# Start of a float32r transformer block on one core: loads in halves, another order of splits and products, eight warming products

## The reference

```
xn   = rms_norm(h, norm1)
proj = xn @ w_in            # q, k, v, z, b, a, sc_c, sc_u, sc_b, gate_a, gate_b
...
q, k, v = split(silu(causal_conv(concat(q, k, v))))
o    = chunk_gated_delta_rule(l2(q), l2(k), v, g, beta)
y_a  = (rms_norm(o) * silu(z)) @ w_dn_out
y_b  = (sc_b * causal_conv(sc_c * sc_u)) @ w_sc_out
h    = h + (sigmoid(gate_a) * y_a + sigmoid(gate_b) * y_b) @ w_o
gt, up = split(rms_norm(h, norm2) @ w_gate_up)
out  = rms_norm(h + (silu(gt) * up) @ w_down, final_norm)
```

## Time and profile before

| | us |
|---|---|
| median of 3 runs | 1045.04 (1044.47 to 1045.52) |
| profiled execution | 1045.25 |
| its span, first to last instruction | 1043.4 |
| TensorE busy | 1028.6 (99%) |
| VectorE, ScalarE, GpSimd busy | 638.4, 486.9, 471.0 |
| mean granted TensorE clock | 0.997 |

### The profile page before, as it was taken

How to read it: one execution, slowest core, us unless ns; L and a number is a source line. 1 busy time by engine, 2 the same in 40 slices (tenths; PEclk the granted TensorE clock), 3 DMA queues, 4 the chain that set the end, 5 groups by cost and what they waited for, 6 DMA issues and landing times.

```text
span 1043.4 us, 22623 instructions
## 1 busy us (share of the span) xinstructions
PE 1028.6 (99%) x9025; PEld 924.2 (89%) x9025; DVE 638.4 (61%) x1141; ACT 486.9 (47%) x1069; POOL 471.0 (45%) x403
## 2 busy tenths in 40 slices
PE   9999999999999999999999999999999999999996
PEld 8989899999999998978888888879999999988886
DVE  6575766767566757563321112699999999972103
ACT  7735454453545353542422233555455555653322
POOL 0163636354454536362554655642322222455553
PEclk9999999999999999999999999999999999999998
DMA  6222212121222121122253233212332332332312
GB/s 230 73 77 73 78 62 78 65 84 63 84 68 75 63 92 63 62 66 78 82 180 121 81 101 101 98 65 96 107 117 94 116 104 100 121 106 97 101 61 81
DMA packets 28825, 95.61 MB, mean 92 GB/s; under 512 B 2984, under 2 KB 5288, under 8 KB 28720
## 3 DMA queue, kind: packets, MB, share of 16 engines
q1 hardware_dynamic: 27520, 91.77, 26.4%
q10 hardware_dynamic: 1200, 2.38, 0.6%
HBM read 92.03 MB, written 2.11 MB: 90 GB/s over the span
## 4 chain that ended last, share of the span: by engine, by line
PE 90%; DVE 5%; ACT 2%; issue 1%; DMA 1%; DVEq 0%; SPq 0%; ACTq 0%
PE bank L1388 90%; DVE pair_sums L1247 1%; DVE og_lo L1226 1%; DVE w_lo L1250 0%; DMA h_in<-h_t 0%; DVE cv L1076 0%; ACT w_hi L529 0%; DVE og_lo L1219 0%; DMA h_in<-gc_dram 0%; PE bank L1588 0%; PE bank L1582 0%; DVE h L1197 0%; DVE raw L905 0%; DVE c L1265 0%; DVE bank L1207 0%
## 5 line engine op out<-in xcount | busy, mean ns | idle before, releaser
L428 POOL TENSOR_TENSOR w_lo<-w_raw,w_hi 128x512 fp32r<-128x512 f32 x202 | 274.6, 1373 | 341.9 <-ACT w_hi L529 341.8
L1388 PE MATMUL bank<-x_hi,w_hi 128*128 128x258 f32 (+2 forms) x896 | 247.6, 334 | 0.4 <-DVE raw L905 0.2
L1388 PE MATMUL bank<-x_hi,w_lo 128*128 128x258 f32 (+2 forms) x896 | 230.4, 315 | 0.0
L1388 PE MATMUL bank<-x_lo,w_hi 128*128 128x258 f32 (+2 forms) x896 | 227.9, 315 | 0.0
L529 ACT ACTIVATE w_hi<-w_raw 128x512 fp32r<-128x512 f32 x278 | 166.6, 622 | 89.9 <-PE bank L1388 86.0
L1388 PEld LDWEIGHTS bank<-x_hi,w_lo 128*128 128x128 f32 x896 | 147.3, 189 | 11.1
L1388 PEld LDWEIGHTS bank<-x_hi,w_hi 128*128 128x128 f32 x896 | 146.3, 189 | 12.2 <-DVE w_lo L916 0.6
L1388 PEld LDWEIGHTS bank<-x_lo,w_hi 128*128 128x128 f32 x896 | 146.3, 189 | 8.8
L1388 PE MATMUL bank<-xe,w_hi 128*128 128x256 f32 (+1 forms) x602 | 123.0, 293 | 2.7 <-DVE t L1212 1.8
L1388 PE MATMUL bank<-og_hi,w_hi 128*128 128x256 f32 (+1 forms) x416 | 124.6, 299 | 0.8 <-DVE w_lo L1250 0.6
L1388 PE MATMUL bank<-og_lo,w_hi 128*128 128x256 f32 (+1 forms) x416 | 123.7, 297 | 0.0
(11 more groups left out here) (306 smaller groups left out, 1827.2 us busy)
## 6 DMA issues: line engine op xcount, KB each, us to landing
w_raw<-w_stream SPq DMA_DIRECT2D x140, 512.0 KB, 3.5
cst<-w_stream SPq DMA_DIRECT2D x22, 512.0 KB, 3.5
h_in<-h_t SPq DMA_DIRECT2D x4, 528.0 KB, 7.1
h<-h_t ACTq DMA_DIRECT2D x1, 2048.0 KB, 11.1
h_in<-gc_dram SPq DMA_DIRECT2D x7, 264.0 KB, 3.1
out<-h SPq DMA_DIRECT2D x4, 256.0 KB, 2.9
out<-h SPq DMA_DIRECT2D x2, 384.0 KB, 2.6
cst<-consts SPq DMA_DIRECT2D x1, 512.0 KB, 8.5
```

Of the source, the lines that this page charges most:

```text
L428: nc.gpsimd.tensor_tensor(low_weights(n)[:, at], raw_weights(n)[:, at], high_weights(n)[:, at].bitcast(f32), ALU.subtract).then_inc(wlo_re ...
L1388: return nc.tensor.matmul(o, w, x, start=start, stop=stop)
```

## The change

The first loads are cut: h tiles 0 and 1 come each by itself, the first two weight blocks in halves, in the order small, w0 first half, h0, h1, w1 first half, h 2-3, w0 second half, h 4-5, w1 second half, h 6-7. ACT and DVE make the weight halves in the order (block 0, first), (1, first), (0, second), (1, second), which `FIRST_HALVES` and `first_half` tell to all who wait; ACT puts the x_hi tiles between them. PE makes the high products of k = 0 and 1 before the low ones of the same block and waits for `whi_ready` for the high ones. `WARM` is 8. The numbers of matmuls, copies and bytes are otherwise the same.

```diff
-WARM = 16
+WARM = 8
+FIRST_HALVES = [(0, 0), (1, 0), (0, 1), (1, 1)]
+def first_half(n, half):
+    return FIRST_HALVES.index((n, half)) + 1 if n < 2 else 2 * n + half + 1
...
             if n < 5:
-                engine.wait_ge(wlo_first, 2 * n + half + 1)
+                engine.wait_ge(wlo_first, first_half(n, half))
...
             sp.dma_start(sm[:, :], small[:, :]).then_inc(small_in, 16)
-            for part in range(4):
+            sp.dma_start(w_raw[:, 0, 0:512], w_stream[0, :, 0:512]).then_inc(w_in[0], 16)
+            sp.dma_start(h_in[:, 0, :], h_t[:, 0, :]).then_inc(h_loaded[0], 16)
+            sp.dma_start(h_in[:, 1, :], h_t[:, 1, :]).then_inc(h_second, 16)
+            sp.dma_start(w_raw[:, 1, 0:512], w_stream[1, :, 0:512]).then_inc(w_in[1], 16)
+            for part in range(1, 4):
                 sp.dma_start(h_in[:, 2 * part:2 * part + 2, :], h_t[:, 2 * part:2 * part + 2, :]).then_inc(h_loaded[part], 16)
-                if part == 0:
-                    for n in range(2):
-                        sp.dma_start(w_raw[:, n, :], w_stream[n, :, :]).then_inc(w_in[n], 16)
+                if part < 3:
+                    n = part - 1
+                    sp.dma_start(w_raw[:, n, 512:1024], w_stream[n, :, 512:1024]).then_inc(w_second[n], 16)
...
             def plain_high(k):
-                act.wait_ge(h_loaded[k // 2], 16)
+                act.wait_ge(h_second if k == 1 else h_loaded[k // 2], 16)
...
-                wait_raw_loaded(act, n)
+                if n < 2 and half:
+                    act.wait_ge(w_second[n], 16)
+                else:
+                    wait_raw_loaded(act, n)
...
             act.wait_ge(small_in, 16)
+            split_weights(0, 0)
             plain_high(0)
             plain_high(1)
-            for n in range(2):
-                split_weights(n, 0)
-                split_weights(n, 1)
-            for k in range(2, KT):
+            split_weights(1, 0)
+            plain_high(2)
+            plain_high(3)
+            split_weights(0, 1)
+            plain_high(4)
+            split_weights(1, 1)
+            for k in range(5, KT):
                 plain_high(k)
...
+            def first_low_half(n, half):
+                at = slice(512 * half, 512 * half + 512)
+                dve.wait_ge(whi_ready, first_half(n, half))
...
             dve.wait_ge(small_in, 16)
-            first_low_weights(0)
-            first_low_weights(1)
+            for n, half in FIRST_HALVES:
+                first_low_half(n, half)
             for k in range(KT):
                 plain_low(k)
...
-                for k, n in [(0, 0), (1, 0), (0, 1), (1, 1)] + [(k, n) for k in range(2, KT) for n in range(2)]:
+                def first_products(k, n, w):
                     parts, to = outs(n)
-                    if k % 4 == 0:
+                    if k % 4 == 0 and w is w_hi:
+                        pe.wait_ge(whi_ready, first_half(n, k // 4))
+                    if k % 4 == 0 and w is w_lo:
                         wait_low(pe, n, k // 4)
                     pe.wait_ge(xhi_ready, k + 1)
-                    for w in (w_hi, w_lo):
-                        for o, s in zip(to, parts):
-                            mm(o, w[:, n, k * 128:(k + 1) * 128], x_hi[:, k, s], start=k == 0 and w is w_hi, stop=False)
+                    for o, s in zip(to, parts):
+                        mm(o, w[:, n, k * 128:(k + 1) * 128], x_hi[:, k, s], start=k == 0 and w is w_hi, stop=False)
+                for n in range(2):
+                    for w in (w_hi, w_lo):
+                        first_products(0, n, w)
+                        first_products(1, n, w)
+                for k in range(2, KT):
+                    for n in range(2):
+                        first_products(k, n, w_hi)
+                        first_products(k, n, w_lo)
```

More of the change, by code:

```diff
@@ L263, in hybrid_block_kernel @@
         h_loaded = [sem(f"h_loaded{part}") for part in range(4)]
+        h_second = sem("h_second")
+        w_second = [sem(f"w_second{n}") for n in range(2)]
         w_in = [sem(f"w_in{slot}") for slot in range(4)]
@@ L909, in plain_low @@
                                                x_hi[:, k, :].bitcast(f32), ALU.mult, ALU.subtract).then_inc(xlo_ready, 1)
-            def first_low_weights(n):
[L911 to L917, removed]
+            def first_low_half(n, half):
+                at = slice(512 * half, 512 * half + 512)
+                dve.wait_ge(whi_ready, first_half(n, half))
+                if n >= 2:
+                    dve.wait_ge(block_done, n - 1)
+                nc.vector.tensor_tensor(w_lo[:, n % 2, at], w_raw[:, n % 3, at], w_hi[:, n % 2, at].bitcast(f32),
+                                        ALU.subtract).then_inc(wlo_first, 1)
+            def first_low_weights(n):
+                first_low_half(n, 0)
+                first_low_half(n, 1)
             def add_square(k):
```

## The result

| | before | after |
|---|---|---|
| median of 12 runs of each on one chip, us | 1045.26 (1044.47 to 1045.52) | 1047.47 (1047.16 to 1047.92) |
| profiled execution / its span, us | 1045.25 / 1043.4 | 1047.6 / 1045.8 |
| mean granted clock | 0.997 | 0.998 |

The ratio after to before is 1.0022, 95% interval 1.0014 to 1.0030: slower, and by 2.2 us where 1.05 were predicted. The range ended at 1047.4, so it missed the median by 0.07. The direction and the way the loss comes about were as predicted; its size was not.

The account below looks back on a forecast made before the run. TensorE, busy 1028.6 of 1043.4 us, was taken to bound the kernel. Start −2.0, operand waits + 0.4 + 0.6, then + 0.64 + 0.27 + 1.12 give about +1.05 us, on 1045.04 a forecast of 1046.1, range 1044.7 to 1047.4.

Parts of the forecast that it names:

- The range: Whole kernel time: 1044.7 to 1047.4 us, given a chance of 0.83 between the tails below 1042.9 and above 1047.1.
- the prediction's sum: PE up to the square sums: −2.0 + 0.4 + 0.6 + 0.64 + 0.27 + 1.12 = about +1.05 us.
- The start: PE's first real product comes at about 6.2 instead of 8.20 us, a gain of 2.0 us.
- VectorE as the path: Before the square sums: x_lo(0) starts 2.19 us later behind the fourth low half; PE waits 1.12 for the last addition.
- The margin of 1.18 us: At the square sums: PE arrives at 22.07, 1.18 us after VectorE's last square addition ends at 20.89.
- the landing term: First loads: at 397 KB per us the nine pieces land from 4.70 to 11.96 us, w1's second half at 10.58.
- Rival 3: First loads: smaller pieces move at a lower rate, w1's second half lands 1.4 us later; time 1047.5, chance 0.13.
- The clock: PE at the start: the sixteen warming matmuls left run at 1.2 GHz, half speed lasting up to about 6.2 us.
- The bound of 10.2 for "costs nothing": PE at the start: a clock rise up to about 10.2 us hides in 2.0 us of waiting.
- Rival 4: PE could stay at 1.2 GHz past 6.2 us; a rise only at 13.4 gives 1047.7; chance 0.06.
- rivals 1 and 2: First: PE keeps its 2.0 us, 1043.0, chance 0.04. Second: DVE's lateness stays within 1.18 us, 1045.0, chance 0.15.
- The lateness is found again at the end: After the square sums: PE's 1.06 us of lateness goes through to the end of the kernel.

Follow-up runs that it names:

- e9: Kernel before, ScalarE's order alone changed: fourth weight half moved from before x_hi 2 to behind x_hi 4; 1046.59 against 1045.09, ratio 1.0015.
- e3: Changed kernel, VectorE's order alone changed: x_lo tiles made between the low halves as inputs come; 1045.69 against 1045.00, ratio 1.0005.
- e10: Kernel before, one VectorE low half of weights some 690 us in moved behind the residual addition and three x sums; 1043.15 against 1045.27, ratio 0.9981.
- e2: Changed kernel with six whole loads, w0 first, instead of nine pieces; 1047.06 against 1045.00, ratio 1.0019.
- e8: e6 with h 0-1 in one load, its other edits the same; 1045.15 against 1045.09, ratio 0.9999.
- e5: Changed kernel with both whole loads, w0 first, and VectorE's x_lo tiles between the low halves; 1046.12 against 1045.19, ratio 1.0008.
- e6: Kernel before, w0 whole first, then h0, h1, w1; VectorE's x_lo 0 and 1 between blocks, PE's x_lo products when ready; 1045.88 against 1045.19, ratio 1.0006.
- e7: Changed kernel with h 0-1 as one load again, weights still in halves; 1047.11 against 1045.19, ratio 1.0017.
- e1: Kernel before with only its first loads cut into nine pieces, in the old order; 1045.52 against 1045.00, ratio 1.0005.
- e4: Changed kernel with sixteen warming products instead of eight; 1047.57 against 1045.00, ratio 1.0025.

## Why the prediction was right in kind and wrong in size

PE's way to the square sums, in the terms of the prediction's sum:

| | before | predicted | after |
|---|---|---|---|
| first real product | 8.20 | 6.2 | 6.26 |
| high part, length | 8.07 | 9.1 | 11.28 |
| x_lo products until the token projections | 3.87 | 4.8 | 4.64 |
| token projections to the square sums | 1.93 | 3.05 | 3.06 |
| square sums start | 22.07 | 23.13 | 25.24 |

**The start was right**: 1.94 of the 2.0 us.

**VectorE as the path was right**, and it is shown, not only argued: e9 makes 1.5 of the 2.2 us with one edit of ScalarE's order, e3 brings the loss down to 0.7 with the loads still late. The margin of 1.18 us, read off, can be tested on six profiles in which PE waits for the last addition. The lateness of x_lo(0), less 1.18, plus the 0.05 from the end of the addition to PE's start, should be PE's own:

| profile | x_lo(0) late by | less 1.18, plus 0.05 | sums late by |
|---|---|---|---|
| after | 4.30 | 3.17 | 3.17 |
| after, second profile | 3.13 | 2.00 | 2.00 |
| sixteen warming products | 3.53 | 2.40 | 2.39 |
| weights in halves | 3.17 | 2.04 | 2.04 |
| whole loads | 2.79 | 1.66 | 1.66 |
| fourth half late alone | 2.42 | 1.29 | 1.29 |
| predicted | 2.19 | 1.06 | 1.06 |

**The step that failed is the landing term**: "By the same line through the landings ... w1 second half 10.58, h 6-7 11.96." It took 397 KB per us, read off whole loads, for the pieces. On the path stands the piece before these, h 4-5: predicted 9.94, landed 4.02 + 8.16 = 12.18. ScalarE's x_hi 4, the fourth half, VectorE's x_lo(0) and PE's sums follow it at the predicted distances, each 2.1 to 2.2 us later than predicted (12.21 for 10.03, 12.89 for 10.71, 14.16 for 12.05, 25.24 for 23.13). In the second profile of the changed kernel it was 0.9 (12.99 for 12.05, 24.07 for 23.13), with h 4-5 at 11.0.

The pieces weren't slower all along. Almost all of the lateness is there when h 2-3 lands, and what comes behind keeps the predicted distances within 0.3 us:

| landing | w1 first half | h 2-3 | h 4-5 | h 6-7 |
|---|---|---|---|---|
| predicted | 6.65 | 7.96 | 9.94 | 11.96 |
| after | 7.37 | 10.14 | 12.18 | 14.25 |
| after, second profile | 6.70 | 8.77 | 11.02 | 13.09 |

Rival 3 named this: w1's second half 1.4 us later, time 1047.5. The half was 2.3 and 1.1 late in the two profiles, and the median is 1047.47. That its number fits so well is partly luck: in the first profile the landing cost more than it said and 0.8 us came back later (below). Its chance of 0.13 was too low. It had been set aside because wba's row was of far shorter runs and one interval of 0.22 us; but the only other support for the line were whole loads, and no row of the kernel before showed a weight load of 256 KB at all. The Trainium skill has a rule against small loads (DMA: Bandwidth & Descriptors, Rules for kernel authors), and the prediction weighed it against the trace by its table's 138 GB/s. The direction of the rule holds here; the 138 GB/s is the row of 64 KB, not one for pieces of 256 KB, and it was a poor measure of them: from 4 to 10 us the loads of the changed kernel moved at 315 and 340 GB/s in its two profiles.

What the pieces cost, from the landing of h 6-7, the same bytes in every kernel:

| loads | landing of h 6-7 in each profile |
|---|---|
| six whole, h 0-1 first (before twice, e9, e10) | 12.0, 11.8, 11.7, 12.0 |
| six whole, w0 first (e2, e8, e5) | 11.7, 12.3, 12.6 |
| h 0 and h 1 apart, w0 first (e6) | 12.9 |
| weights in halves, w0 first (e7) | 13.1 |
| nine pieces, h first (e1) | 13.2 |
| nine pieces, w0 first (after twice, e3, e4) | 14.2, 13.1, 13.4, 13.5 |

Whole and nine pieces don't overlap, and the cleanest pair, e1 against the first row, differs by 1.2 to 1.5 us. But two profiles with exactly the same whole loads (e2, e5) differ by 1.0, and with w0 first the landings scatter in every form, with h 0-1 first and whole they don't. So the order may have a share beside the size; no run separates them. Why the loads come late is not settled. The packet records give part of it: a 2 KB packet takes 84 ns in the median and a 4 KB packet 159, which on 16 engines is 390 against 412 GB/s, some 0.2 us over the 1552 KB; the rest is packets that took longer than the median, and not the small ones alone. Between 4 and 14 us the mean of the 2 KB packets in the changed kernel is 97 ns. The packets of loads of two h tiles (4224 bytes, uncut by the change) have a median of 164 ns in both kernels, but a mean of 166 before and 194 after. The traces don't say what held them up.

**The clock** was predicted at full speed by 10 us; in the first profile it came between 10.9 and 11.4 (two products of 258 columns take 0.64 us at 10.95, 0.40 at 11.43), in the second at about 7.3. The bound of 10.2 for "costs nothing" was passed in the first, and it cost nothing (e4), since the operands were later still. Rival 4 falls, and rivals 1 and 2 with the sum.

**"The lateness is found again at the end"** held only in part: 3.17 us at the sums, 2.35 at the end of that profiled execution. Some 0.1 us of it was back by 60 us, the rest came back at 690 us. There GpSimd and VectorE both make a low half of weights. Kernel before, GpSimd and then VectorE:

```profile
689.02 1.31 POOL L432 TENSOR_TENSOR w_lo<-w_raw,w_hi 128x512 fp32r<-128x512 f32 x1
```

```profile
689.10 1.78 DVE L1250 TENSOR_TENSOR w_lo<-pair_sums,w_hi 128x512 fp32r<-128x512 f32 x1
```

Changed kernel, GpSimd, VectorE, and the PE row that waits for `t`:

```profile
692.84 1.59 POOL L441 TENSOR_TENSOR w_lo<-w_raw,w_hi 128x512 fp32r<-128x512 f32 x1 [0.46 <-ACT w_hi L538]
```

```profile
692.59 0.68 DVE L1268 TENSOR_TENSOR w_lo<-pair_sums,w_hi 128x512 fp32r<-128x512 f32 x1
```

```profile
695.22 0.50 PE L1406 MATMUL bank<-xe,w_hi 128*128 128x256 f32 x2 [0.30 <-DVE t L1230]
```

Where GpSimd begins 0.08 us ahead, VectorE's operation takes 1.78 us and ends 0.55 after GpSimd's. Where VectorE begins 0.25 ahead, it takes 0.68, and GpSimd's takes 1.59. PE's wait for `t` is 1.8 in the one and 0.3 in the other. That is 1.5 won; 0.8 of it had been lost just before (PE's lateness is 3.08 at 640 us, 3.90 at 690 and 2.40 at 696), most of it where 512-column products between 657 and 690 us started 0.233 us apart instead of 0.229 (cause open). The second profile of the changed kernel and that of e9 show the same. e2, e4 and e7 show no such return: their lateness at the sums of 1.7, 2.4 and 2.0 is 2.0, 2.4 and 2.4 at the end. So which of the two operations comes first is decided by a tenth of a microsecond, and small changes far ahead can turn 0.7 us either way. The range had no room for it.

The forecast's +1.05 then becomes: 2.11 more from the landing, 0.8 less behind the sums, +2.35 in this execution, and +2.2 between the medians.

## What to carry to other kernels

When a copy moves back in one engine's written order, look at the in-order queue of the engine that consumes it: everything behind that consumer moves too, here 4.3 us of lateness against 1.18 of margin, and interleaving the consumer in the order of arrival took most of it back. A load that is cut must be priced with its own landing row; where none exists, give "later by a microsecond or two" a real chance. And before mending a start whose gain may only be waited for later, read the longest waits elsewhere: one moved operation at 690 us was worth as much as this whole change lost.

## What the hardware showed that was not expected

- The mean granted clock was 0.998, higher than before, in a run whose matmuls were at half pace until about 11 us: four products of 264 columns take 1.08 us at 9.65, two of 258 take 0.40 at 11.43. The prediction's reading of 0.997 as "half speed for some 6.3 us, up to about 6.2" was wrong: that its 6.2 us meets the change of pace there is luck. In the kernel before the lower of the two levels (granted clock 0.50, 1.2 GHz) is reported at the end of the execution, behind TensorE's last work; rows of windows (us, PE busy, granted clock, DMA share, GB/s):

```profile
4.00:5.00 1.00, 1.00 (x7) 1.00 0.99 403
...
1036.00:1037.00 1.00, 0.61 (x2) 1.00 0.00 0
1038.00:1043.40 5.40, 0.00 (x0) 0.50 0.57 194
```

  The stretch from 4 to 5 us is given as 1.00, though its seven matmuls start 0.21 us apart and those behind 6.2 us 0.11. Only the pace of the matmuls themselves tells the level at the start.
- A VectorE operation with two SBUF inputs took 1.78 us instead of 0.68 when a GpSimd operation had begun 0.08 us before it, and GpSimd's 1.59 instead of 1.31 in the other order, while VectorE's `h<-bank,h`, one input in PSUM, kept its 0.68 beside GpSimd's 689.00 start in e10. From the first start to the last end the pair takes 1.86 and 1.84 us, against 1.31 + 0.68 = 1.99 one behind the other: they nearly take turns. The Trainium skill says so (SBUF — State Buffer, Who interferes with whom: a VectorE instruction with two SBUF inputs contends with a GpSimd instruction that reads SBUF, and the order of issue decides which of them blocks), and the trace agrees: the one that begins second lasts longer than it does alone, VectorE's by 1.10 us and GpSimd's by 0.28.
- The same loads, issued in the same order, landed up to 1.0 us apart in two kernels (e2, e5) and 1.2 us apart in two executions of one.
